# Two chained transformer blocks on one core: first groups of stages take the inner dimension tile by tile over four units, with only the last four tiles unit by unit

## The reference, cut to what matters

```python
h = x + nsa_mixer(rms_norm(x), ...)                  # its output projection: stage wo
h = h + square(relu(rms_norm(h) @ ffn_w1)) @ ffn_w2  # 2048 -> 8192 -> 2048: stages ff0..ff3, fd0..fd3
gate = sigmoid(rms_norm(h) @ ple_w_gate)             # stage gate
h = h + (p @ ple_w_proj) * gate
h = rms_norm(h)                                      # end of the first block
m = swa_sink_attention(rms_norm(h), ...)             # its keys: stage k2; its output projection: stage wo2
h = h + rms_norm(m)
u = conv3(rms_norm(h) @ w_up)                        # 2048 -> 11264: stages up0..up2
h = h + rms_norm((silu(gate half of u) * value half of u) @ w_down)   # stages dn0..dn2
```

## Time and profile before

| | |
|---|---|
| median of 3 runs | 2322.53 us (2320.23 to 2323.21) |
| the profiled execution: its time | 2323.18 us |
| its span, first to last instruction | 2321.4 us |
| mean granted TensorE clock | 0.986 of full speed |
| PE busy | 2238.7 us (96%) |
| DVE busy | 1609.9 us (69%) |
| ACT busy | 1097.9 us (47%) |
| POOL busy | 752.4 us (32%) |
| weights read | 401.64 MB in 757 pieces of 512 KB |

### The profile page before, as it was taken

One profiled execution on the slowest core, in us unless ns is written; L12 is line 12 of the kernel. 1 busy time (PEld: TensorE's weight loads), 2 busy tenths in 40 slices (PEclk: granted clock), 3 DMA queues, 4 the chain that ended last, 5 costly groups with the idle time before them and its releaser, 6 DMA issues.

```text
span 2321.4 us, 38150 instructions
## 1 busy us (share of the span) xinstructions
PE 2238.7 (96%) x12956; PEld 1953.8 (84%) x12956; DVE 1609.9 (69%) x2001; ACT 1097.9 (47%) x1627; POOL 752.4 (32%) x751
## 2 busy tenths in 40 slices
PE   8999889999999999999999999979999999999995
PEld 7888758888888888888899877867888888888885
DVE  7676575656666666666687666787785678767876
ACT  5344354544454354354466455454553455434552
POOL 4121003452142142133445122235540154413433
PEclk9999899999999999999999999989999999999998
DMA  6557204555555555555555643534555555555552
GB/s 238 181 176 238 93 1 151 190 179 199 187 187 188 189 190 189 190 182 190 181 191 182 207 167 126 172 119 150 203 190 191 189 188 184 190 190 190 190 189 92
DMA packets 115141, 407.34 MB, mean 175 GB/s; under 512 B 12464, under 2 KB 16848, under 8 KB 115056
## 3 DMA queue, kind: packets, MB, share of 16 engines
q1 hardware_dynamic: 110592, 401.64, 51.2%
q10 hardware_dynamic: 4464, 4.61, 0.7%
HBM read 404.05 MB, written 2.15 MB: 175 GB/s over the span
## 4 chain that ended last, share of the span: by engine, by line
PE 87%; DVE 6%; POOL 3%; issue 2%; ACT 2%; DMA 0%; POOLq 0%; SPq 0%; DVEq 0%; ACTq 0%
PE bank L406 49%; PE bank L413 26%; PE bank L420 1%; PE bank L422 1%; PE bank L421 1%; PE bank L506 1%; DVE wboth L771 1%; POOL bias L1580 1%; PE bank L465 1%; PE bank L467 1%; PE bank L466 1%; ACT Sm L1313 1%; PE bank L678 1%; DVE Sm L1198 1%; ACT wboth L1268 0%
## 5 line engine op out<-in xcount | busy, mean ns | idle before, releaser
L771 DVE TENSOR_TENSOR wboth<-raw,wboth 128x1024 fp32r<-128x1024 f32 x757 | 1033.7, 1367 | 446.8 <-ACT wboth L1268 446.1
L1268 ACT CAST wboth<-raw 128x1024 fp32r<-128x1024 f32 x757 | 788.2, 1048 | 773.4 <-PE bank L406 383.0
L406 PE MATMUL bank<-A,wboth 128*128 128x512 f32 x3200 | 775.5, 394 | 14.8 <-DVE A L846 9.1
L406 PEld LDWEIGHTS bank<-A,wboth 128*128 128x128 f32 x3200 | 590.4, 190 | 134.1 <-issue 16.6
L406 PE MATMUL bank<-H,wboth 128*128 128x512 f32 x2304 | 558.4, 392 | 0.3 <-DVE z L802 0.3
L406 PEld LDWEIGHTS bank<-H,wboth 128*128 128x128 f32 x2304 | 421.6, 189 | 84.0 <-issue 3.4
L413 PEld LDWEIGHTS bank<-A,wboth 128*128 128x128 f32 x3200 | 413.9, 192 | 29.9 <-DVE wboth L771 6.9
L413 PE MATMUL bank<-A,wboth 128*128 128x256 f32 x3200 | 421.9, 284 | 9.9 <-DVE wboth L771 5.5
L413 PEld LDWEIGHTS bank<-H,wboth 128*128 128x128 f32 x2304 | 298.9, 191 | 14.2 <-issue 1.0
L413 PE MATMUL bank<-H,wboth 128*128 128x256 f32 x2304 | 305.4, 283 | 0.0
L802 DVE TENSOR_REDUCE z<-bank 128x256 f32<-128x512 f32 x284 | 195.7, 689 | 88.8 <-PE bank L406 86.9
(11 more groups left out here) (219 smaller groups left out, 1611.6 us busy)
## 6 DMA issues: line engine op xcount, KB each, us to landing
raw<-wstream SPq DMA_DIRECT2D x757, 512.0 KB, 3.2
bias<-bias_rows ACTq DMA_DIRECT2D x6, 512.0 KB, 5.1
x<-xT SPq DMA_DIRECT2D x4, 512.0 KB, 6.8
out<-x SPq DMA_DIRECT2D x3, 512.0 KB, 2.7
pA<-bias_rows ACTq DMA_DIRECT2D x2, 512.0 KB, 8.6
out<-x SPq DMA_DIRECT2D x2, 256.0 KB, 2.0
Sm<-pT ACTq DMA_DIRECT2D x1, 256.0 KB, 2.6
con<-consts SPq DMA_DIRECT2D x1, 254.0 KB, 10.2
```

The source lines that it names most:

```text
L406: last = nc.tensor.matmul(bank(j)[:, :], whi[:, s, cols(i)], moving(j, k), start=(k == 0), stop=(k == K - 1))
L771: V.tensor_tensor(wlo[:, s, :], raw[:, s, :], whi[:, s, :].bitcast(F32), ALU.subtract).then_inc(lo_ready, 1)
L1268: C.copy(whi[:, s, :], raw[:, s, :]).then_inc(hi_ready, 1)
```

## The change

Only the cuts of a mixed group change. Where it had three cuts (tiles 0 to 3, 4 to 7, 8 to K-1), it now has one cut for each of the tiles 0 to K-5, and one with the last four tiles. Since the matrix engine's loop, `ends` and the packing of the weights on the host all call `order`, they follow. `wo2` keeps its own cuts.

```diff
-def order(n, K, mixed=0, first=((0, 4), (4, 8), (8, None))):
+def order(n, K, mixed=0, first=None):
     out = []
     for g in range(0, n, 4):
         js = range(g, min(g + 4, n))
-        cuts = first if g // 4 < mixed else ((0, K),)
-        out += [(j, k) for a, b in cuts for j in js for k in range(a, b or K)]
+        cuts = [(0, K)]
+        if g // 4 < mixed:
+            cuts = first or [(k, k + 1) for k in range(K - 4)] + [(K - 4, K)]
+        out += [(j, k) for a, b in cuts for j in js for k in range(a, b)]
     return out
```

## The result

Median 2354.32 us (4 runs, 2353.71 to 2356.32), against 2321.38 us before (4 runs, 2319.95 to 2323.21): ratio 1.0143, 95% interval 1.0128 to 1.0158. The change makes the kernel slower by 1.4%.

The account below looks back on a forecast made before the run. The matrix engine, busy 96% of the span, was taken as the bound, so only its waits and clock count. Input gains, bank waits, paired unit ends and 9.4 us of clock summed to +33.7 us: 2356 us, range 2336 to 2371.

Parts of the forecast that it names:

- Banks at the head of a stage: All four banks needed within 0.7 us of a group's start: losses of 1.5 (`ff0`), 3.1 (`fd0`), 2.5 us (`gate`).
- Units in pairs make DVE late: Ends of `wo`, `fd3`, `ff0`: last emptying starts about 5.6, not 3 us after; next heads lose 2.2, 2.3, 2.7 us more.
- The rival that it doesn't grow at all: DVE ends stages as late as now because pairs flow through POOL and ACT quickly: +19 us, 2342 us; chance 0.27.
- Stalls inside the pairs: Split of piece 12 late behind four units' work: 0.6 us each in `wo` and `fd3`, 1.3 us in `ff0`.
- Smaller heads: Heads of `fd1` to `fd3` and `dn0` to `dn2`: a bank wait of 0.3 us each, 1.7 us in all.
- `dn2`, `v2`, `kv`: Bank waits inside `dn2` lose 5.1 us, one more split ahead of `v2` 1.2; later inputs in `kv` gain 1.5.
- Clock: Half-clock stretches behind three long waits and one in `up0`: 5.5 times 1.7 us, 9.4 us; bounds 1 and 8 stretches.
- `up0`: Later inputs gain about 4.5 us by piece 7; norm, banks and paired convolutions return it: 1.0 us loss, clock apart.
- What the profile would show: L408 waits for `z` some 25 us, over 5 at `ff0`, `fd0`; `dn2` wait pairs 1.7; L415 waits near piece 12.

Follow-up runs that it names:

- Experiment 2: Changed kernel, but only tiles 0 to 7 go tile by tile, so units end one per piece as before; 2340.93 us, ratio 1.0081 to the kernel before.
- experiment 3: Changed kernel plus unread matmuls (20, 20, 17) filling the waits for unit 3's bank at the heads of `ff0`, `fd0` and `gate`; 2345.75 us.
- experiment 1: Changed kernel, but mixed groups open with the old cut of tiles 0 to 3; units still end in pairs; 2332.84 us, ratio 1.0051 to the kernel before.
- Experiment 4: Kernel before, with the new cuts only in the first group of `kv` and the first group of `up0`; 2323.00 us, ratio 1.0005.
- 5: Kernel of Experiment 4, with DVE's additions for the norm sum of `up0` two pieces earlier; 2320.11 us, ratio 0.9991 to the kernel before.
- experiment 7: Kernel of run 5, plus twelve unread matmuls into bank 7 ahead of the norm of `up0`; 2319.77 us, ratio 0.9988 to the kernel before.
- 8: Kernel of experiment 6, plus nine unread matmuls into bank 7 ahead of `v2`; 2317.52 us, ratio 0.9982 to the kernel before.
- experiment 6: Kernel before, with new cuts only in the first group of `kv` and DVE's additions in `up0` two pieces earlier; 2319.43 us, ratio 0.9989.

## Why the prediction was right

The time (2356 us predicted, 2354.3 measured) came out by the mechanism that the prediction named, and its terms, one by one, were mostly near. Against the 32.6 us that the pieces give, the sum has some 4 us too much (the lateness at the heads, the stalls in `wo` and `fd3`) and some 3 us too little (`ff0` inside, the smaller heads, `up0`, `dn2`, `kv`). That it comes out within 1 to 2 us is in part luck.

- *Banks at the head of a stage.* Right. Experiment 2 shows this term nearly alone: waits of 3.05 and 3.33 us, where the prediction worked out 3.2 and 3.4 from the earlier trace rows.
- *Units in pairs make DVE late.* Right in kind, too large in size: predicted emptyings that start 5.6 us after the stage, measured 4.85, 5.00 and 4.57. Clock apart, the heads cost 2.8, 4.5 and 4.3 us (measured less what experiment 3 gave back) instead of 3.7, 5.4 and 5.2: 0.9 us too much each time. The mis-sized steps are the 2.2, 2.3 and 2.7 us for the lateness. The prediction let it grow to the most that four slots of weights allow; it grew by 1.7 us. The rival that it doesn't grow at all is out by experiments 1 and 2. One slip is in the sum for `ff0`: a wait of 5.7 us less the 1.70 that the norm absorbs is 4.0 us, not 3.7.
- *Stalls inside the pairs.* 0.6 us each in `wo` and `fd3`: 0 measured. 1.3 in `ff0`: 1.9, in two waits of 0.89 and 0.34 us in L408 near pieces 12 and 14 and what surrounds them. `wo`'s estimate was 0.4 us away from no stall at all, and fell on the other side.
- *Smaller heads.* 1.7 us predicted for six; 2.65 measured. The wait shown is as small as expected (0.19 us in `fd1`), but each costs 0.4 to 0.5 us of the piece's start. Where the other 0.2 to 0.3 us go I haven't shown.
- *`dn2`, `v2`, `kv`.* Predicted 5.1, measured 5.4; 1.2 and 1.1; -1.5 and -1.05. In `kv` the half-clock stretch at 25.78 is gone, as hoped, but two waits (0.59 and 0.41 us) remain; by experiment 2 the later inputs, from which the term started, add little to it.
- *Clock.* Right in size by two misses that cancel. The prediction took 1.5 stretches of 3.4 us for each long wait at half their length, 2.55 us: 2.66, 2.47 and 2.57 us were given back in experiment 3. But the stretches were two such lengths each (6.83 us), and half of that would be 3.4 us; they cost less, among other things because 0.9 to 1.2 us of each lay in the wait itself. "TensorE: Matmul & The Clock Gate" in the Trainium skill (Loop structure matters more than you think) says that DVE's copying out of PSUM doesn't cool the engine, but it says so of a loop whose next matmuls follow immediately. The prediction left that condition out when it set the page against its clock term. Here the next matmuls had to wait 4.08 to 4.89 us for DVE's emptying, so these runs don't contradict the page, and its words gave no reason to take 9.4 us off the sum. Filling these very waits with matmuls took the stretches away.
- *`up0`.* The step whose mechanism failed: 1.0 + 1.7 us for the clock, measured 3.3. The 2.7 and the 3.3 us are near each other, the way there isn't. The prediction saw that the norm waits for DVE's seven additions, and thought that they would come some 3 us earlier. They came 0.9 us earlier: they ended 32.5 us after the first product matmul of `up0` (1601.57 - 1569.08), before 33.4 us (1579.21 - 1545.78). So the wait grew from 2.18 to 6.27 us, half clock lay around it, and the lead of 5 us was gone and 1 us more. Experiment 4 shows the same with the first group alone (5 us of lead, 2.6 us of loss in the end). The larger part of the loss, 2.3 of the 3.3 us, comes only from piece 16 on: a wait of 3.13 us for a bank, of which some is regained because the kernel before waits longer for splits behind it. The prediction named its cause, the convolutions in pairs in the second group, but gave it no price of its own. The gain of later inputs in `up0` came neither by the cuts alone (4) nor, beyond 0.5 us by pieces, with an earlier sum (5, 7), since a split is late next.
- *What the profile would show.* The long waits are where they were foretold, if below 5 us each, but L408's waits for `z` are 13.3 us in six, not some 25. That figure contradicted the prediction's own terms, which give 5.7 + 5.4 + 1.7 = 12.8 us for them. And of the 13.3 us only 10.2 are at the heads that these terms stand for; 3.13 are at piece 16 of `up0`. `dn2`'s pairs of waits are 1.24 us by the profile, not 1.7, while each costs 1.8 us of the pieces' starts. No waits for splits stand near piece 12 of `wo` and `fd3`, and those in `ff0` are L408's, not L415's.

## What to carry to other kernels

Before you open as many accumulators as there are banks, look at how long after a stage's start its predecessor's last bank is emptied; the earliest matmul on that bank can't be before it. And count where units end: two that end together cost the engines behind them time that shows mostly later, at the next stage's head. An order that helps at one place (`kv`, 1.05 to 2.03 us in all nine traces that have new cuts there) is best used there alone; a wait that can't be moved can be filled with matmuls into an unused bank, which pays where the matrix engine sets the pace behind it (experiments 3 and 8) and not where another engine does (7).

## What the runs showed of the hardware

The half-clock stretch near 240 us, in a stage that no kernel here changes, isn't equally long in each execution. Windows of the changed kernel (the stretch alone), of experiment 3 and of experiment 7 (20 us around it); behind the span stand PE, PEld, DVE, ACT and POOL busy, PEclk, DMA share and GB/s:

```profile
239.61:253.26 13.65, 13.65 (x54) 12.59 (x54) 0.00 (x0) 0.00 (x0) 0.00 (x0) 0.50 0.12 38
```

```profile
235.00:255.00 20.00, 20.00 (x108) 17.71 (x107) 6.12 (x9) 4.05 (x6) 0.00 (x0) 0.83 0.23 77
```

```profile
235.00:255.00 20.00, 20.00 (x94) 18.15 (x93) 3.21 (x3) 3.07 (x4) 0.00 (x0) 0.66 0.15 54
```

A mean of 0.66 over 20 us is 13.7 us at 0.50, one of 0.83 is 6.8 us. The same work thus takes up to 3.4 us more or less (94 matmuls fit into the one window, 108 into the other), and the ten traces show three lengths: 13.7 us in four, 10.2 in two, 6.8 in four. By its size this could be most of the spread of 4 us between the runs of one kernel; the times of runs without a trace can't show it. So two profiled spans that differ by 3 us say nothing by themselves: compare them place by place, as the table above does, and take small differences from many runs. What decides the length I haven't found.

The length of a wait alone doesn't tell either whether a half-clock stretch follows. The wait for a bank at piece 16 of `up0` was 3.13 us in the changed kernel, and the eight matmuls behind it took 2.11 us, full clock; in experiment 1 it was 3.15 us, and they took 3.42 us in a stretch at 0.50. Behind the wait of 1.62 us for tile 15 in `up0` the same eight matmuls, first of the kernel before, then of experiment 6 (where a further wait of 0.83 us stood 3 us ahead):

```profile
1566.80 2.00 PE L406 MATMUL bank<-A,wboth 128*128 128x512 f32 x8
```

```profile
1561.96 3.35 PE L410 MATMUL bank<-A,wboth 128*128 128x512 f32 x8
```

So one stretch behind one wait in one trace can be chance. The claims above rest on more: all three stretches of experiment 3 went at once and the median fell by 8.6 us, and the stretch at the head of `v2` is in each of the nine traces without its filler.
